# The closing stage of a hybrid convolution and MoE layer: last expert rows of two tiles read in two steps, and the sample tile summed ahead of tile 3

## The chip, the cores and the metric

One core of a Trainium2 chip runs the whole kernel. The metric is device time in microseconds of one execution, as the median of several runs. Five engines work side by side and wait for each other by semaphores: TensorE (PE), VectorE (DVE), ScalarE (ACT), GpSimd (POOL) and SyncE (SP). SP issues most DMA transfers, in the order of its program, and waits at an instruction until its semaphores allow it.

## The reference

The kernel computes one layer for 512 prompt tokens and 8 sample tokens, 1024 features wide: a token mixer of two convolution branches, then a mixture of 64 experts in which every token uses 8, and one shared expert. What matters here is the end of it:

```python
def moe_tokens(h, p):
    ...
    _, eidx = lax.top_k(jnp.where(emask, sel, -jnp.inf), TOP_K)
    w = jnp.take_along_axis(scores, eidx, axis=1)
    w = w / jnp.sum(w, axis=-1, keepdims=True) * ROUTED_SCALE
    ...
    act = jax.nn.silu(hg) * hu * gate[:, :, None].astype(h.dtype)
    routed = jnp.einsum('tef,efd->td', act, p['w2'])
    shared = (jax.nn.silu(h @ p['ws1']) * (h @ p['ws3'])) @ p['ws2']
    return routed + shared
...
    f = lax.map(lambda hs: moe_tokens(hs, p), h)
    x = x + gt2 * rmsnorm(f, p['g_post2'])
```

For each token, the outputs of its 8 experts are weighted and added, the shared expert's output is added, the sum is normalised by its root mean square, scaled by a gate and added to the residual.

## The kernel before

The 520 tokens make five tiles: tiles 0 to 3 of 128 prompt tokens, and tile 4 with the 8 sample tokens (`TT` is 5). The expert phase runs in passes. One pass takes two strips of 64 token rows, each of one expert: POOL gathers the rows, PE multiplies them with the expert's weights (L1746, L1754, L1760), ACT evicts the result (L973), and POOL scatters it to `y_rows` in DRAM (L624). The experts go in ascending order.

`y_rows` holds 8 rows for each token, in two halves. Half 0 of a tile holds its tokens' four latest choices (0 is the latest expert of a token, so the last to be computed) and half 1 its four earlier ones. A half of a full tile is 512 rows of 4 KB, 2 MB.

The closing stage brings them back and sums them. SP reads them in the order of its program, each read behind `rows_there(n)`, which loads a pass number from `few` and waits until that pass's rows have been written to DRAM: number 0 guards half 1 of all tiles, number 1 + i guards half 0 of tile i. The pass numbers are found in the routing: `last_of` collects the places of each tile's latest rows, PE transposes it and DVE takes the maximum (L1281, L1282, L1727, L1315, L1357). `y_first` are the buffers for half 1 and `y_last` those for half 0, in slots of the expert weights that are no longer needed (`slot_free(e)` waits for that). Tile 3's half 0 goes where tile 0's half 1 was, so it also waits for `early_pe`. `ysmp` takes the sample's 64 rows.

PE sums in PSUM. For the n-th tile in `order`, in the banks of `bank_of[n]`: `shared_down(n)` (L1819) adds the shared expert, `gated_rows(n, h, src)` (L1852) adds the four rows of half h with their gates, and `last_sums(n)` does so for half 0 as soon as it has landed. The sample's rows have a product of their own (L1878). Each full sum releases ACT (`stat_mm`): a square with a sum over columns (L1003) and a root (L1006). DVE takes the reciprocal (L1402), multiplies the sum in PSUM by it and by the gate (L1408, which counts `yacc`) and adds the residual (L1411, which counts `fin_out`). SP then stores the tile (L468). ACT, DVE and SP take the tiles in the order n = 0 to 4. `outb` has three buffers, so the fourth and the fifth tile wait for the stores of the first and the second.

Of the kernel before, what the change touches and what calls it, by code (L numbers as in the profile page):

```python
# [10 lines left out]
ALU = mybir.AluOpType  # L11
ACT = mybir.ActivationFunctionType
AX = mybir.AxisListType
ds = bass.ds

P = 128
# [6 lines left out]
def build_program(  # L23
# [8 lines left out]
    NP = x_prompt.shape[1]  # L32
    NS = x_sample.shape[0]
    T = NP + NS
# [4 lines left out]
    TT = (T + P - 1) // P  # L39
    LAST = T - (TT - 1) * P  # L40
    TOPK, NG, TOPG = 8, 8, 4
# [10 lines left out]
    y_rows = nc.dram_tensor("y_rows", (T * TOPK, D), F32, kind="Internal").ap()  # L52
# [4 lines left out]
    with ctx:  # L57
# [98 lines left out]
        y_first = [split] + [whole(t) for t in (slot_part(5, 0, YF), slot_part(0, 0, YF), slot_part(1, 0, YF))]  # L156
        y_last = [whole(t) for t in (slot_part(2, 0, YF), slot_part(3, 0, YF), slot_part(4, 0, YF))] + [split]
# [4 lines left out]
        ysmp = slot_part(3, YF + D, D)[0:NS * TOPK, :]  # L162
        outb = [hflat[:, D:2 * D], slot_part(4, YF, D), slot_part(4, YF + D, D)]

        ident = sb("ident", [P, P])
# [66 lines left out]
        first_at, steps_of, used_by, half_of, few = (table[:, n, :] for n in range(5))  # L232
        gidx = sb("gidx", [P, 8], I32)
        sidx = sb("sidx", [P, 6], I32)
        red = sb("red", [P, 4])
        nrm = sb("nrm", [P, 2, TT])
        last_of = nrm[:, :, :].rearrange("p a n -> p (a n)")[:, 0:1 + TT]
        kv = sb("kv", [P, TT, TOPK])
        m4 = sb("m4", [P, 4])
        bm = sb("bm", [P, P // 4])  # L240
# [2 lines left out]
        gcol, gpart_s, gcol_s, gmat_s = rs[:, 384:416], rs[0:NS * TOPK, 416:420], rs[0:NS * TOPK, 420:421], rs[0:NS * TOPK, 424:424 + NS]  # L243

        ps = ctx.enter_context(nc.psum_tensor("ps", [P, 8, 512], F32))
# [31 lines left out]
        S = {n: sem(n) for n in names}  # L277
# [2 lines left out]
        y_out = [sem(f"y_out{b}") for b in range(2)]  # L280
        y_first_in = sem("y_first_in")
        y_last_in = [sem(f"y_last_in{b}") for b in range(TT - 1)]
        order = tuple(range(TT))
        tile_out = [sem(f"tile_out{b}") for b in range(3)]
        g2_out, g2_in = sem("g2_out"), sem("g2_in")
        bank_of = (6, 0, 2, 4, 6)
        smp_in = sem("smp_in")

        LA = 7
# [8 lines left out]
        def _(sp):  # L298
# [119 lines left out]
            def tile_rows(dst, i, h, landed):  # L418

                at = i * P * TOPK + h * P * TOPK // 2  # L420
                for part, n in dst[i]:
                    sp.dma_start(part.rearrange("p (b d) -> p b d", b=n),
                                 y_rows[at:at + n * P, :].rearrange("(b p) d -> p b d", p=P)).then_inc(landed, 16)
                    at += n * P
# [8 lines left out]
            def rows_there(n):  # L433

                passes_gone = sp.value_load(few[0:1, 4 + n:5 + n], min_val=4, max_val=STEPS + 3)
                sp.wait_ge(S["yb_free"], passes_gone)
                passed()
# [9 lines left out]
            x1_back(TT - 1)  # L447
            sp.wait_ge(g2_out, 16)
            sp.dma_start(G2, g2_rows[0:1, :].to_broadcast([P, D])).then_inc(g2_in, 16)
            rows_there(1)  # L450
            tile_rows(y_last, 0, 0, y_last_in[0])
            slot_free(E - 2)
            sp.dma_start(G2s, g2_rows[1:NSEQ, :]).then_inc(g2_in, 16)
            rows_there(2)
            tile_rows(y_last, 1, 0, y_last_in[1])
            rows_there(3)
            slot_free(E - 1)
            tile_rows(y_last, 2, 0, y_last_in[2])
            rows_there(4)
            sp.wait_ge(S["early_pe"], 1)  # L460
            tile_rows(y_last, 3, 0, y_last_in[3])
            rows_there(TT)
            sp.dma_start(ysmp, y_rows[NP * TOPK:T * TOPK, :]).then_inc(smp_in, 16)
            for n in range(TT):
                i = order[n]
                sp.wait_ge(S["fin_out"], n + 1)
# [542 lines left out]
        def _(dve):  # L1009
            counts = {}  # L1010

            def link(ins, name=None, wait=True):

                key = name or "dve_step"
                counts[key] = counts.get(key, 0) + 1
                ins.then_inc(S[name] if name else dve_step, 1)
                if wait:
                    dve.wait_ge(S[name] if name else dve_step, counts[key])

            tt, ts, stt = dve.tensor_tensor, dve.tensor_scalar, dve.scalar_tensor_tensor  # L1020
# [47 lines left out]
            with dve.Fori(0, C // 2) as it:  # L1068
                for jj in range(2):
                    j = it * 2 + jj  # L1070
                    n = [0]
# [139 lines left out]
            for i in range(2, TT):  # L1211
                n, b = (P if i < TT - 1 else LAST), (0, 2, 6, 0, 2)[i]
# [13 lines left out]
            gs, g8, gi, gm, gneg, t8, wk8, wsum, wk9, val8 = (s8(n) for n in range(10))  # L1226
# [4 lines left out]
            for i in range(TT):  # L1231
                for q in range(NG):
                    link(dve.max(out=top[:, q, 8 * i:8 * i + 8], in_=sel[:, i, q * EG:(q + 1) * EG]),
                         wait=(i == TT - 1 and q == NG - 1))
# [5 lines left out]
            for i in range(TT):  # L1240
                link(dve.match_replace(out=gm[:, i, :], in_to_replace=g8[:, i, :], in_values=gs[:, i, :], imm_value=2 * NEG),
                     wait=(i == TT - 1))
# [5 lines left out]
            for i in range(TT):  # L1248
                link(dve.match_replace(out=repl[:, i, :], in_to_replace=t8[:, i, :], in_values=selm[:, i, :], imm_value=2 * NEG),
                     wait=(i == TT - 1))  # L1250
# [29 lines left out]
            link(ts(below, incl, 1.0 / STRIP, slotid[:, 0:1], ALU.mult, ALU.is_le))  # L1280
            link(dve.tensor_reduce(last_of[:, 0:1], val8[:, :, 4], AX.X, ALU.max), wait=False)  # L1281
            link(dve.tensor_copy(last_of[:, 1:1 + TT], val8[:, :, 0]), wait=False)  # L1282
            link(dve.tensor_reduce(first_strip, below, AX.X, ALU.add))
            link(ts(first_strip, first_strip, E - 1.0, None, ALU.min), "es_dve")
            dve.wait_ge(S["idx_mm"], 1)
# [26 lines left out]
            link(ts(one64[0:1, :], beyond, RING - 1.5, 2.0 * R, ALU.is_gt, ALU.mult))  # L1312
            link(ts(beyond, beyond, 1.0, float(SLOT), ALU.add, ALU.mult))
            link(tt(first_at, beyond, one64[0:1, :], ALU.add), "table_dve")
            link(dve.tensor_reduce(red[0:1 + TT, 2:3], ps[0:1 + TT, 6, 0:P], AX.X, ALU.max), "early_dve", wait=False)  # L1315
            tile_no = dve.alloc_register("tile_no")
            dve.reg_mov(tile_no, 0)

# [33 lines left out]
                              in_=xgs[u].rearrange("p (g r k) -> p g k r", g=4, k=C)[:, :, 4 * h:4 * h + 4, :]).then_inc(S["xe_dve"], 1)  # L1352

            dve.wait_ge(S["es_pe"], 2)
            last_pass = few[:, 4:5 + TT]
            link(ts(last_pass, ps[0:1, 6, P:P + 1 + TT], 4.0 * P - 1.0, None, ALU.add), "early_dve")
            link(ts(last_pass, last_pass, 7, None, ALU.logical_shift_right), "last_pass_dve", wait=False)  # L1357
            dve.wait_ge(S["sh_mm"], 2 * FT)
            for h in range(2):
# [37 lines left out]
            for n in range(TT):  # L1397
                i, f = order[n], bank_of[n]
# [15 lines left out]
        def _(pe):  # L1414
            def mark(ins, name):
                ins.then_inc(S[name], 1)

            mm, tr = pe.matmul, pe.transpose
            pe.wait_ge(consts, 12)
            pe.wait_ge(crow_in, 48)  # L1420
            for c in range(C):
                ins = tr(ps[:, 5, c * NS:(c + 1) * NS], x_stok[:, c * P:(c + 1) * P], ident[0:NS, 0:NS])
            mark(ins, "xs_pe")
            pe.wait_ge(S["csilu_act"], 1)
            for c in range(C):
                ins = tr(ps[:, 4, c * NSEQ:(c + 1) * NSEQ], c_tok[:, c * P:(c + 1) * P], ident[0:NSEQ, 0:NSEQ])
            mark(ins, "cT_pe")
            pe.wait_ge(x_in, 16)
            for c in range(C):
                if c >= 4:  # L1430
                    pe.wait_ge(S["xT_act"], c - 4 + 1)
                for i in range(TT - 1):
                    ins = tr(ps[:, c % 4, i * P:(i + 1) * P], x_tok[:, i, c * P:(c + 1) * P], ident[:, :])
# [8 lines left out]
            for c in range(C):  # L1442
                pe.wait_ge(S["xsq_dve"], c + 2)
                ins = quarter_stat(6, hT[:, c, :], c)
# [279 lines left out]
                             stop=(i == TT - 1 and k == TOPK - 1))  # L1724
            ins.then_inc(S["idx_mm"], 1)
            pe.wait_ge(S["es_dve"], 1)
            mm(ps[0:1 + TT, 6, 0:P], last_of, ident[:, :], start=True, stop=True)  # L1727
            mm(ps[0:1, 6, 3 * P:4 * P], red[:, 0:1], ident[:, :], start=True, stop=True).then_inc(S["es_pe"], 1)
            pe.wait_ge(S["hx_done"], TT)
            pe.wait_ge(S["idx_dve"], 1)  # L1730
# [31 lines left out]
                return ins  # L1762

            pe.wait_ge(S["early_dve"], 1)
            mm(ps[0:1, 6, P:P + 1 + TT], red[0:1 + TT, 2:3], ident[0:1 + TT, 0:1 + TT], start=True, stop=True).then_inc(S["es_pe"], 1)
            at_step = pe.alloc_register("step_pe")
            pe.reg_mov(at_step, 0)
            entries = table[:, :, :].rearrange("a n e -> a (n e)")
# [44 lines left out]
            def shared_down(n):  # L1813

                i, f = order[n], bank_of[n]
                rows = P if i < TT - 1 else LAST
                for h in range(2):
                    for k in range(FT):
                        mm(ps[0:rows, f + h, :], scr[:, 2 + k, i * P:i * P + rows], ws2_in[k][:, h * 512:(h + 1) * 512],  # L1819
                           start=(k == 0), stop=False)  # L1820
# [24 lines left out]
            def gated_rows(n, h, src):  # L1845

                i, f = order[n], bank_of[n]
                for c in range(2):
                    for b in range(4):
                        part, n = src[i][0] if b < src[i][0][1] else src[i][1]  # L1850
                        at = b % n * D + c * 512
                        ins = mm(ps[32 * b:32 * b + 32, f + c, :], gmat[:, b, i, h, :], part[:, at:at + 512],  # L1852
                                 start=False, stop=(h == 0))
                return ins

            def last_sums(n):
                pe.wait_ge(y_last_in[order[n]], 16 * len(y_last[order[n]]))
                mark(gated_rows(n, 0, y_last), "stat_mm")

            pe.wait_ge(S["gm_dve"], 2)  # L1860
# [1 line left out]
            pe.wait_ge(y_first_in, 16 * TT)  # L1862
            mark(gated_rows(0, 1, y_first), "early_pe")
            gated_rows(1, 1, y_first)
            pe.wait_ge(S["xe_dve"], passes * 2 + 2)
            last_sums(0)
            pe.wait_ge(S["ex_yd"], passes + 2)
            shared_down(3)
            last_sums(1)
            gated_rows(2, 1, y_first)  # L1870
            last_sums(2)
            gated_rows(3, 1, y_first)
            pe.wait_ge(S["yacc"], 1)
            shared_down(TT - 1)
            last_sums(TT - 2)
            pe.wait_ge(smp_in, 16)
            for c in range(2):
                ins = mm(ps[0:NS, bank_of[TT - 1] + c, :], gmat_s, ysmp[:, c * 512:(c + 1) * 512], start=False, stop=True)  # L1878
            mark(ins, "stat_mm")


_INS = ['x_prompt', 'x_sample', 'state_sconv', 'state_cconv', 'c_prompt', 'c_sample', 'w_ada', 'b_ada',
# [23 lines left out]
```

## Time and profile before

| | before |
|---|---|
| median of 3 runs | 1244.65 us |
| lowest and highest run | 1244.25 and 1246.88 us |
| the profiled execution | 1245.29 us |
| its span, first to last instruction | 1243.5 us |
| TensorE busy | 1170.2 us, 94% |
| VectorE, ScalarE, GpSimd busy | 45%, 26%, 42% |
| mean granted TensorE clock | 0.975 of full speed |

The profile is of one execution; the medians come from runs without it. Times in its rows count from the span's start. A busy share is a mean over stages of different kinds, so the last 35 us are read from their own rows. The durations of matmuls overlap, since they are pipelined: what a block costs is the time from its start to the start of the next.

### The profile page before, as it was taken

To read this page: it belongs to the slowest core of one execution; us is meant where nothing else is said; L and a number is where in the kernel's file an instruction comes from. 1 tells how busy PE (TensorE), PEld (TensorE's weight loads), DVE (VectorE), ACT (ScalarE), POOL (GpSimd) and SP (SyncE) were. 2 spreads that over 40 slices of the span, in tenths; PEclk is the share of its full clock that TensorE was granted. 3 is DMA by queue.
4 is the path that set the end of the run, shared out by engine and by line. 5 is a ranking of instruction groups with operands and counts; after the bars stand their busy time and mean duration, and the time that the engine had idled before them with its cause. 6 is when DMAs were issued, how large, how long until landed. Compare 5 with 4: busy or idle time off the path is not lost.

```text
span 1243.5 us, 26196 instructions
## 1 busy us (share of the span) xinstructions
PE 1170.2 (94%) x9253; PEld 848.0 (68%) x9254; DVE 562.0 (45%) x912; ACT 327.3 (26%) x620; POOL 523.6 (42%) x527
## 2 busy tenths in 40 slices
PE   4899999999999899979899999997989999899897
PEld 3699999999999899967655555554445555455442
DVE  3285667658568868127733422221112222222134
ACT  3523322322333441335211111111111111111122
POOL 2144444445448244310654445443344454354420
PEclk9899999999999899988999999998989999999999
DMA  9954344424421232437779999999999999999977
GB/s 313 323 168 153 99 137 152 151 85 152 152 84 34 69 101 88 133 142 307 288 283 391 392 393 413 411 412 416 413 414 411 410 414 401 412 414 413 352 288 271
DMA packets 149033, 337.45 MB, mean 271 GB/s; under 512 B 14807, under 2 KB 99363, under 8 KB 123369
## 3 DMA queue, kind: packets, MB, share of 16 engines
q1 hardware_dynamic: 129304, 296.57, 63.4%
q0 software_dynamic: 16656, 34.14, 7.3%
q10 hardware_dynamic: 3025, 6.07, 1.4%
q8 instruction: 34, 0.56, 0.2%
q14 instruction: 14, 0.11, 0.0%
HBM read 322.21 MB, written 33.30 MB: 286 GB/s over the span
## 4 chain that ended last, share of the span: by engine, by line
PE 73%; DMA 13%; DVE 6%; issue 5%; POOL 1%; SPq 1%; ACT 1%; DVEq 0%; POOLq 0%; ACTq 0%
PE ps L1746 24%; PE ps L1760 10%; DMA w<-in_w_dram 10%; PE ps L1509 10%; PE ps L1510 10%; PE ps L1511 10%; DMA ring<-in_w_ada_dram 2%; PE ps L1754 2%; PE ps L1819 1%; PE ps L1522 1%; PE ps L1852 1%; PE ps L1451 1%; PE ps L1527 1%; DVE sg L1152 1%; DVE rs L1129 1%
## 5 line engine op out<-in xcount | busy, mean ns | idle before, releaser
L1746 PE MATMUL ps<-w,xe 128*64 (+1 forms) x3136 | 381.1, 395 | 25.7 <-DMA w<-in_w_dram 20.2
L1746 PEld LDWEIGHTS ps<-w,xe 128*64 128x64 f32 x3136 | 223.3, 137 | 177.7 <-issue 63.2
L534 POOL TENSOR_TENSOR wsplit<-ring,wsplit 128x1024 fp32r<-128x1024 f32 x80 | 194.4, 2430 | 281.5 <-ACT wsplit L687 251.4
L1509 PE MATMUL ps<-h_s_hi,wsplit 128*128 128x260 f32 x960 | 272.2, 283 | 0.0
L1511 PE MATMUL ps<-h_s_hi,wsplit 128*128 128x260 f32 x960 | 270.7, 282 | 0.0
L1510 PE MATMUL ps<-h_lo_m_hi,wsplit 128*128 128x260 f32 x832 | 234.8, 282 | 0.0
L1371 DVE TENSOR_TENSOR rs<-sg,ps 128x128 f32<-128x128 f32 x98 | 28.2, 288 | 371.2 <-ACT sg L985 371.2
L1509 PEld LDWEIGHTS ps<-h_s_hi,wsplit 128*128 128x128 f32 x960 | 180.6, 188 | 6.7 <-issue 5.9
L1760 PE MATMUL ps<-w,eactT 128*64 128x512 f32 (+1 forms) x784 | 185.0, 592 | 0.0
L1511 PEld LDWEIGHTS ps<-h_s_hi,wsplit 128*128 128x128 f32 x960 | 180.8, 188 | 0.0
L687 ACT ACTIVATE wsplit<-ring 128x1024 fp32r<-128x1024 f32 x80 | 84.8, 1060 | 296.8 <-PE ps L1511 286.5
L1510 PEld LDWEIGHTS ps<-h_lo_m_hi,wsplit 128*128 128x128 f32 x832 | 156.6, 188 | 0.0
L1098 DVE SCALAR_TENSOR_TENSOR ps<-conv,vecs,ps 128x512 f32<-128x512 f32 x224 | 154.7, 745 | 0.0
L613 POOL DMA_INDIRECT conv<-h_rows,gidx x100 | 101.8, 1018 | 44.4 <-issue 24.6
L613 POOL DMA_INDIRECT scr<-h_rows,gidx x100 | 101.6, 1016 | 42.8 <-issue 22.9
L1760 PEld LDWEIGHTS ps<-w,eactT 128*64 128x64 f32 x784 | 54.3, 136 | 64.6 <-issue 54.1
L608 POOL COPY gidx<-tail 128x4 int32 (+1 forms) x50 | 10.2, 205 | 186.8 <-DVE xe L1351 183.7
L973 ACT ACTIVATE act<-ps 128x1024 f32<-128x1024 f32 x50 | 51.2, 1024 | 115.5 <-PE ps L1760 112.6
L985 ACT ACTIVATE sg<-ps 128x128 f32<-128x128 f32 x98 | 27.2, 277 | 199.6 <-PE ps L1746 199.6
L987 ACT ACTIVATE eactT<-ps 128x128 f32<-128x128 f32 x98 | 27.2, 277 | 172.6 <-PE ps L1754 172.6
L1351 DVE STREAM_TRANSPOSE xe<-scr 128x512 f32<-128x512 f32 x50 | 55.9, 1120 | 35.3 <-PE ps L1746 31.3
L1351 DVE STREAM_TRANSPOSE xe<-conv 128x512 f32<-128x512 f32 x50 | 56.2, 1123 | 32.8 <-PE ps L1746 32.8
(333 smaller groups left out, 1343.9 us busy)
## 6 DMA issues: line engine op xcount, KB each, us to landing
w<-in_w_dram SPq DMA_DIRECT2D x192, 1024.0 KB, 22.5
ring<-in_w_in_dram SPq DMA_DIRECT2D x56, 512.0 KB, 3.8
ring<-in_w_ada_dram SPq DMA_DIRECT2D x8, 2048.0 KB, 8.8
ring<-in_w_ada_dram SPq DMA_DIRECT2D x8, 1024.0 KB, 12.5
ring<-y_rows SPq DMA_DIRECT2D x4, 2048.0 KB, 17.0
ring<-in_w_out_a_dram SPq DMA_DIRECT2D x8, 512.0 KB, 4.1
ring<-in_w_out_b_dram SPq DMA_DIRECT2D x8, 512.0 KB, 4.1
ring<-in_w_o_dram SPq DMA_DIRECT2D x8, 512.0 KB, 4.2
```

The lines of the kernel that those rows point to most:

```text
L534: pool.tensor_tensor(wsplit[:, b, 1], raw[raw_slot], wsplit[:, b, 0], ALU.subtract).then_inc(S["w_lo"], 1)
L613: pool.indirect_dma_start(out=xgs[u][:, g * QR:(g + 1) * QR], out_offset=None, in_=h2_rows.rearrange("t (q d) -> (t q) d", q=4), in_offset ...
L687: act.activation(wsplit[:, b, 0], raw[raw_slot], ACT.Copy).then_inc(S["w_hi"], 1)
L973: act.activation(yb[:, 1 - u, :], ps[:, 4:6, :].rearrange("p b n -> p (b n)"), ACT.Copy).then_inc(S["ex_yd"], 1)
L1098: chain(stt(out=acc[k % 2] if k != KC - 2 else cvj, in0=glu[:, k:k + NP], scalar=vecs[:, ds(j + (V_WC + 8 * k), 1)], in1=acc[k % 2], op0=A ...
L1351: dve.transpose(out=xe[:, 4 * h:4 * h + 4, :].rearrange("p k (g s) -> p g k s", g=4), in_=xgs[u].rearrange("p (g r k) -> p g k r", g=4, k= ...
L1371: tt(eact[:, cols], esil[:, cols], ps[:, 2 + f, P:2 * P], ALU.mult).then_inc(S["ex_mul"], 1)
L1509: mm(ps[:, bank + h, 0:HT], wsplit[:, b, 0, k, :], hi[:, k, p:q], start=(k == 0), stop=False)
L1510: mm(ps[:, bank + h, 0:HT], wsplit[:, b, 0, k, :], lo[:, k, p:q], start=False, stop=False)
L1511: ins = mm(ps[:, bank + h, 0:HT], wsplit[:, b, 1, k, :], hi[:, k, p:q], start=False, stop=(k == C - 1))
L1746: ins = mm(ps[a * STRIP:(a + 1) * STRIP, 2 + f, 0:2 * P], xe[:, k, a * STRIP:(a + 1) * STRIP], w[a][:, f, k], start=(k == 0), stop=(k == C ...
L1760: ins = mm(ps[a * STRIP:(a + 1) * STRIP, 4 + h, :], eactT[:, k, a * STRIP:(a + 1) * STRIP], w[a][:, k, h * 512:(h + 1) * 512], start=(k == ...
```

## The change

`EARLY` is 2: for tiles 0 and 1 the routing also records the place of each token's choice 2, so that SP has two pass numbers more (numbers 6 and 7 of `rows_there`). Half 0 of these two tiles is read by choice: `choice_rows(i, (2, 3))` reads choices 2 and 3 behind the new pass number, `choice_rows(i, (0, 1))` reads choices 0 and 1 behind the old one. Each choice is a transfer of its own, 128 rows of 4 KB to every fourth partition. The tiles' buffers end up as before.

The order of the finish becomes tiles 0, 1, 2, the sample, tile 3; the two change banks. PE adds tile 2's and tile 3's halves 1 at other places, adds the sample's rows behind tile 2's last sums, and ends with tile 3's last sums. SP reads the sample's rows ahead of tile 3's.

```diff
-        last_of = nrm[:, :, :].rearrange("p a n -> p (a n)")[:, 0:1 + TT]
+        EARLY = 2
+        MARKS = 1 + TT + EARLY
+        last_of = nrm[:, :, :].rearrange("p a n -> p (a n)")[:, 0:MARKS]
...
-        order = tuple(range(TT))
+        order = (0, 1, 2, TT - 1, TT - 2)
...
-        bank_of = (6, 0, 2, 4, 6)
+        bank_of = (6, 0, 2, 6, 4)
...
-            rows_there(1)
-            tile_rows(y_last, 0, 0, y_last_in[0])
+            def choice_rows(i, choices):
+
+                part, at = y_last[i][0][0], i * P * TOPK
+                for k in choices:
+                    sp.dma_start(part[k::TOPK // 2].rearrange("t (b d) -> t b d", b=4),
+                                 y_rows[at:at + P * TOPK // 2, :].rearrange("(b t k) d -> k t b d", b=4, k=TOPK // 2)[k]
+                                 ).then_inc(y_last_in[i], 16)
+
+            rows_there(1 + TT)
+            choice_rows(0, (2, 3))
             slot_free(E - 2)
             sp.dma_start(G2s, g2_rows[1:NSEQ, :]).then_inc(g2_in, 16)
+            rows_there(2 + TT)
+            choice_rows(1, (2, 3))
+            rows_there(1)
+            choice_rows(0, (0, 1))
             rows_there(2)
-            tile_rows(y_last, 1, 0, y_last_in[1])
+            choice_rows(1, (0, 1))
             rows_there(3)
             slot_free(E - 1)
             tile_rows(y_last, 2, 0, y_last_in[2])
+            rows_there(TT)
+            sp.dma_start(ysmp, y_rows[NP * TOPK:T * TOPK, :]).then_inc(smp_in, 16)
             rows_there(4)
             sp.wait_ge(S["early_pe"], 1)
             tile_rows(y_last, 3, 0, y_last_in[3])
-            rows_there(TT)
-            sp.dma_start(ysmp, y_rows[NP * TOPK:T * TOPK, :]).then_inc(smp_in, 16)
...
             link(dve.tensor_copy(last_of[:, 1:1 + TT], val8[:, :, 0]), wait=False)
+            link(dve.tensor_copy(last_of[:, 1 + TT:MARKS], val8[:, 0:EARLY, 2]), wait=False)
...
             def last_sums(n):
-                pe.wait_ge(y_last_in[order[n]], 16 * len(y_last[order[n]]))
+                i = order[n]
+                pe.wait_ge(y_last_in[i], 16 * (TOPK // 2 if i < EARLY else len(y_last[i])))
...
             gated_rows(1, 1, y_first)
+            gated_rows(2, 1, y_first)
             pe.wait_ge(S["xe_dve"], passes * 2 + 2)
             last_sums(0)
             pe.wait_ge(S["ex_yd"], passes + 2)
+            shared_down(4)
+            gated_rows(4, 1, y_first)
+            last_sums(1)
+            pe.wait_ge(S["yacc"], 1)
             shared_down(3)
-            last_sums(1)
-            gated_rows(2, 1, y_first)
             last_sums(2)
-            gated_rows(3, 1, y_first)
-            pe.wait_ge(S["yacc"], 1)
-            shared_down(TT - 1)
-            last_sums(TT - 2)
             pe.wait_ge(smp_in, 16)
             for c in range(2):
-                ins = mm(ps[0:NS, bank_of[TT - 1] + c, :], gmat_s, ysmp[:, c * 512:(c + 1) * 512], start=False, stop=True)
+                ins = mm(ps[0:NS, bank_of[3] + c, :], gmat_s, ysmp[:, c * 512:(c + 1) * 512], start=False, stop=True)
             mark(ins, "stat_mm")
+            last_sums(4)
```

PE's end in the kernel before, the first row of each block from tile 3's shared expert on. L1819 is a shared block, L1852 sums of four rows (`y_last_in` with a tile's number is the wait for half 0; the row without a wait is tile 3's half 1), L1878 the sample's rows:

```order
L1819 MATMUL ps<-act,scr 128x512 [waits ex_yd]
L1852 MATMUL ps<-ring,act 32x512 [waits y_last_in1]
L1852 MATMUL ps<-act 32x512 [waits y_last_in2]
L1852 MATMUL ps<-ring,act 32x512 x8
L1819 MATMUL ps<-act,scr 8x512 [waits yacc]
L1852 MATMUL ps<-act 32x512 [waits y_last_in3]
L1878 MATMUL ps<-ring,rs 8x512 [waits smp_in]
```

PE's end in the changed kernel, from the same block on; its lines 1834, 1867 and 1893 are the lines 1819, 1852 and 1878 of before:

```order
L1834 MATMUL ps<-act,scr 128x512 [waits ex_yd]
L1867 MATMUL ps<-ring,act 32x512 x8
L1867 MATMUL ps<-ring,act 32x512 [waits y_last_in1]
L1834 MATMUL ps<-act,scr 8x512 [waits yacc]
L1867 MATMUL ps<-act 32x512 [waits y_last_in2]
L1893 MATMUL ps<-ring,rs 8x512 [waits smp_in]
L1867 MATMUL ps<-act 32x512 [waits y_last_in3]
```

The sample's shared block now stands ahead of tile 2's last sums, and tile 3's last sums stand behind the sample's rows, at the end.

DVE's last two finishes in the kernel before, tile 3 and then the sample (8 rows):

```order
L1408 SCALAR_TENSOR_TENSOR act<-ps,nrm,ring 128x1024 [waits tile_out0,dve_step]
L1411 TENSOR_TENSOR act<-act,ring 128x1024 [waits yacc]
L1402 RECIPROCAL nrm<-nrm 8x1 [waits root_act]
L1408 SCALAR_TENSOR_TENSOR act<-ps,nrm,ring 8x1024 [waits tile_out1,dve_step]
L1411 TENSOR_TENSOR act<-act,ring 8x1024 [waits yacc]
```

The same place in the changed kernel:

```order
L1423 SCALAR_TENSOR_TENSOR act<-ps,nrm,ring 8x1024 [waits tile_out0,dve_step]
L1426 TENSOR_TENSOR act<-act,ring 8x1024 [waits yacc]
L1417 RECIPROCAL nrm<-nrm 128x1 [waits root_act]
L1423 SCALAR_TENSOR_TENSOR act<-ps,nrm,ring 128x1024 [waits tile_out1,dve_step]
L1426 TENSOR_TENSOR act<-act,ring 128x1024 [waits yacc]
```

The finish with 8 rows has changed places with tile 3's, and so have the two stores that follow them on SP.

## Rows read from the trace of the kernel before

**Rows 1.** Page: its first line, and the chain that ended last, by engine.
```profile
span 1243.5 us, 26196 instructions
PE 73%; DMA 13%; DVE 6%; issue 5%; POOL 1%; SPq 1%; ACT 1%; DVEq 0%; POOLq 0%; ACTq 0%
```
**Rows 2.** Chain of waits in order of time (start, us, what): two pieces.
```profile
1209.51 3.70 PE ps L1819 x8
...
1239.97 1.21 DVE act L1411
```
**Rows 3.** Timeline of PE, 1209 to 1236 us: start, busy us, instructions, idle before.
```profile
1209.51 3.70 PE L1819 MATMUL ps<-act,scr 128*128 128x512 f32 x8 [0.27 <-DVE rs L1395]
1213.14 3.64 PE L1852 MATMUL ps<-act 128*32 128x512 f32 x32
1216.60 1.90 PE L1852 MATMUL ps<-ring,act 128*32 128x512 f32 x16
1218.43 3.70 PE L1819 MATMUL ps<-act,scr 128*128 128x512 f32 x8
...
1228.95 3.17 PE L1819 MATMUL ps<-act,scr 128*8 128x512 f32 x7
1231.53 0.63 PE L1852 MATMUL ps<-act 128*32 128x512 f32 x3
...
1234.20 1.88 PE L1878 MATMUL ps<-ring,rs 64*8 64x512 f32 x4
```
**Rows 4.** Line L422, loads issued at 1211.1, 1220.9, 1181.0: each with its landing.
```profile
L422 SPq DMA_DIRECT2D act<-y_rows x1: 360/360/360, 1211.1 to 1211.1; - x1
DMA to landing us min/median/max: 12.5/12.5/12.5
...
L422 SPq DMA_DIRECT2D act<-y_rows x1: 487/487/487, 1220.9 to 1220.9; - x1
DMA to landing us min/median/max: 8.4/8.4/8.4
...
L422 SPq DMA_DIRECT2D ring<-y_rows x1: 1330/1330/1330, 1181.0 to 1181.0; - x1
DMA to landing us min/median/max: 22.6/22.6/22.6
```
**Rows 5.** Timeline of ACT and DVE from 1234 us: tile 3, then the sample.
```profile
1234.35 1.02 ACT L1003 ACTIVATE scr<-ps 128x1024 f32<-128x1024 f32 x1 [5.42 <-PE ps L1852]
1236.03 1.28 DVE L1408 SCALAR_TENSOR_TENSOR act<-ps,nrm,ring 128x1024 f32<-128x1024 f32 x1
1238.67 1.27 DVE L1408 SCALAR_TENSOR_TENSOR act<-ps,nrm,ring 8x1024 f32<-8x1024 f32 x1
1239.97 1.21 DVE L1411 TENSOR_TENSOR act<-act,ring 8x1024 f32<-8x1024 f32 x1
```
**Rows 6.** Line L468, the five stores, and SP's wait at the end.
```profile
L468 SPq DMA_DIRECT2D out_dram<-act x5: 332/333/380, 1222.9 to 1241.2; - x5
DMA to landing us min/median/max: 2.6/3.1/8.5
...
SPq L472 <- DMA out_dram<-act: 1.5, 1, 1.5
```
**Rows 7.** Timeline of SP, its last issues ahead of tile 2's load.
```profile
1188.91 0.34 SPq L449 DMA_DIRECT2D ring<-g_rows  x1
1200.23 0.37 SPq L422 DMA_DIRECT2D ring<-y_rows  x1
1201.37 0.32 SPq L453 DMA_DIRECT2D ring<-g_rows  x1
1209.30 0.38 SPq L422 DMA_DIRECT2D ring<-y_rows  x1
```
**Rows 8.** Timeline of DVE in the routing: the copy, and what waits behind it.
```profile
607.38 0.16 DVE L1282 COPY nrm<-act 128x5 f32<-128x5 f32 x1
...
608.10 0.23 DVE L1286 COPY tok<-ps 128x66 f32<-128x66 f32 x1 [0.25 <-PE ps L1723]
```

More of the change, by code:

```diff
@@ L1314, in _ @@
             link(tt(first_at, beyond, one64[0:1, :], ALU.add), "table_dve")
-            link(dve.tensor_reduce(red[0:1 + TT, 2:3], ps[0:1 + TT, 6, 0:P], AX.X, ALU.max), "early_dve", wait=False)
+            link(dve.tensor_reduce(red[0:MARKS, 2:3], ps[0:MARKS, 6, 0:P], AX.X, ALU.max), "early_dve", wait=False)
             tile_no = dve.alloc_register("tile_no")
@@ L1354, in _ @@
             dve.wait_ge(S["es_pe"], 2)
-            last_pass = few[:, 4:5 + TT]
-            link(ts(last_pass, ps[0:1, 6, P:P + 1 + TT], 4.0 * P - 1.0, None, ALU.add), "early_dve")
+            last_pass = few[:, 4:4 + MARKS]
+            link(ts(last_pass, ps[0:1, 6, P:P + MARKS], 4.0 * P - 1.0, None, ALU.add), "early_dve")
             link(ts(last_pass, last_pass, 7, None, ALU.logical_shift_right), "last_pass_dve", wait=False)
@@ L1726, in _ @@
             pe.wait_ge(S["es_dve"], 1)
-            mm(ps[0:1 + TT, 6, 0:P], last_of, ident[:, :], start=True, stop=True)
+            mm(ps[0:MARKS, 6, 0:P], last_of, ident[:, :], start=True, stop=True)
             mm(ps[0:1, 6, 3 * P:4 * P], red[:, 0:1], ident[:, :], start=True, stop=True).then_inc(S["es_pe"], 1)
@@ L1764, in _ @@
             pe.wait_ge(S["early_dve"], 1)
-            mm(ps[0:1, 6, P:P + 1 + TT], red[0:1 + TT, 2:3], ident[0:1 + TT, 0:1 + TT], start=True, stop=True).then_inc(S["es_pe"], 1)
+            mm(ps[0:1, 6, P:P + MARKS], red[0:MARKS, 2:3], ident[0:MARKS, 0:MARKS], start=True, stop=True).then_inc(S["es_pe"], 1)
             at_step = pe.alloc_register("step_pe")
```

## Prediction

> **What bounds the kernel now.** I read the page's head first: of the chain that ended last TensorE holds 73% and the DMA 13% [rows 1]. That is an average over a projection stage, the routing, 49 expert passes and a closing stage. The change touches little outside the last stage, so only that stage counts. The chain of waits in order of time shows it as one stretch: a PE block that starts at 1209.51 us, after the last expert pass, and then PE to the very end of its own work, followed by ScalarE and VectorE [rows 2]. From 1209.51 us on no row of the chain is a DMA.
>
> The timeline of PE gives that stretch block by block [rows 3]. The reader is to see that each block starts where the one before it ends: the shared expert of one tile (L1819, 8 matmuls) takes 3.63 us from start to start, a half of four expert rows (L1852, 16 matmuls) 3.46 / 2 = 1.73 us, or 1.83 us when a shared block follows (1216.60 to 1218.43). The sample tile's shared block and the sums behind it take 5.25 us together (1228.95 to 1234.20), although the sample has 8 rows: its matmuls cost the same 0.43 us each as those of a full tile. Then the sample's own rows, 4 matmuls, 1.88 us with their end. No block names a DMA as what it waited for. The first block starts when VectorE has made the gate matrix, which the change leaves alone.
>
> Were the loads late, it would show there. They are close but not late. Tile 2's last rows were issued at 1211.1 us and landed 12.5 us later, at 1223.6; PE took them up at 1225.5, which is 1.73 + 1.73 us ahead of 1228.95. The second piece of tile 3's last rows went at 1220.9 and landed 8.4 us later, at 1229.3; its first sums stand at 1231.53 [rows 3, 4]. So in the kernel before the loads have some 2 us in hand.
>
> Behind PE stands the finish of a tile: a square-sum and a root on ScalarE, then a reciprocal and two passes over 1024 columns on VectorE (L1408, L1411). For tile 3 ScalarE starts at 1234.35 and L1408 at 1236.03, 1.68 us later. The sample's L1408 starts 2.64 us after that and its L1411 ends at 1241.18 (1239.97 + 1.21) [rows 5]. The sample's finish is as long as a full tile's, because it is as many columns wide. Its output of 32 KB is issued at 1241.2; the issue takes 0.33 us and SP waits 1.5 us more [rows 6]: 1.8 us from issue to landing.
>
> **The change part by part.** *The reads in two steps.* SP gets eight loads of 512 KB for tiles 0 and 1 in place of two of 2 MB, so six issues more, of 0.37 us like the one at 1200.23, and two more looks at a pass number, at most 0.77 us each (1200.23 + 0.37 to 1201.37, which holds another wait too): 3.8 us of SP in all. They lie where SP waits anyway, between 1188.91 and 1209.30 [rows 7]; only the two issues of tile 1's later half stand right ahead of tile 2's load, 0.4 us. What moves: 1 MB of tile 0 and 1 MB of tile 1 may be read before 1209 us instead of around it. If none of it went earlier, the loads would land as they did, and those were in time. Tile 0's last sums stand at 1218.3 us now (below), so a half read as late as 1201.4 and landing in 12.5 us is still in time. So the edit frees transfers that no instruction waited for: its gain is 0, and the cover that hides its cost is SP's idle time. If that cover were gone, tile 2's load would go 3.8 us later and land at 1227.4.
>
> *The order on PE.* The same blocks run in another order, so PE's sum stays, but for one more step from sums to a shared block (0.1 us). From 1209.51: shared tile 2 3.63, three first halves 5.19, tile 0's last sums 1.83, shared tile 3 3.63, its first half 1.73, tile 1's last sums 1.83, the sample's shared block with tile 2's last sums 5.25. That is 1232.60. Then the sample's rows 1.72 (4 x 0.43) to 1234.3 and tile 3's last sums to 1236.0, 1236.2 with their end. Every load is wanted later than before: tile 2's at 1230.9 instead of 1225.5, tile 3's at 1234.3 instead of 1231.5. The sample's shared block waits for VectorE to have read tile 0's bank. Tile 0's sums end at 1220.2, 1.7 us of ScalarE and 1.3 us of L1408 behind that is 1223.2, and the block stands at 1227.3, so this wait costs 0.
>
> *The finish.* Here the order costs. Before, tile 2 is done by the time tile 3's sums end, and two finishes queue on VectorE. Now tile 2's sums, the sample's and tile 3's end at 1232.6, 1234.3 and 1236.2, 1.7 to 1.9 us apart, and each finish takes 2.64 us. Three of them queue. ScalarE starts 0.15 us after the next block does (1234.20 to 1234.35), so tile 2's L1408 stands at 1232.60 + 0.15 + 1.68 = 1234.43, the sample's at 1237.07, tile 3's at 1239.71. Its L1411 ends 2.51 us after that (1238.67 to 1241.18 in the row of before): 1242.22, against 1241.18. **That is +1.0 us.** Tile 3's root is ready at 1237.9, so VectorE, not PE, sets the end. The bound below: if nothing queued ahead of tile 3, its L1408 would start at 1236.2 + 1.68 and the end would be 1240.4, a gain of 0.8 us. I take +1.0, since all three durations are rows.
>
> *The last output.* The last store is now tile 3's 512 KB instead of the sample's 32 KB. The shortest landing among the five outputs, 2.6 us, is that of tile 3 in the kernel before, with no load beside it; the median is 3.1 us [rows 6]. Against 1.8 us that is +0.8 us, at most +1.3 us; I take **+0.8 us**, the one alone on the queue. The Trainium skill (DMA: Bandwidth & Descriptors, section "Anatomy of one DMA — SWDGE (gpsimd) path") gives a fit of 2.0 us plus the bytes at 436 GB/s, for another way of issuing; by that estimate the two stores take 3.2 and 2.1 us, the difference is 1.1 us, and the sum would be 0.3 us higher. The row decides.
>
> *The third part* is a copy of two more columns of the routing (about as long as L1282, 0.16 us), and two rows more in a transpose and a maximum. VectorE idles 0.25 us for PE right behind that place [rows 8], so it costs 0, at most 0.2 us.
>
> **Sum.** +1.0 + 0.8 = +1.8 us on a span of 1243.5 us: 1245.3 us. The profiled execution took 1245.29 us with its span and all around it, so 1247.1 us in its terms. It lay 0.64 us above the median of the runs, 1244.65 us, so the median to expect is **1246.4 us**. Two times of this kernel within 0.2%, 2.5 us, can't be told apart with confidence, and +1.8 us lies within that.
>
> **The rivals.** *A: the small loads land late (slower).* The place is tile 1's last sums, wanted at 1225.5, whose later half can't be issued before 1209.3. It decides if that half needs more than 16 us. For it: each of the small loads writes only every fourth partition, a shape that the trace of before does not have, and one load of the same rows needed 22.6 us when issued at 1181.0 with others ahead [rows 4]; that would stall PE by 6.4 us and give 1252.8 us. Against it: 1 MB is half of what landed in 12.5 us in the same crowd, and 2 MB fewer stand around it. The Trainium skill speaks for it (DMA: Bandwidth & Descriptors, "Measured (HBM→SBUF, 128 partitions, SWDGE, issued from GpSimd)"): it asks for at least 1 MiB a load for three quarters of the peak, and the trace of before shows no landing of a 512 KB load beside others by which to tell whether that holds here. 7 in 100.
>
> *B: the loads were the limit after all (faster).* Two us in hand are little, and in runs without a profile PE may have waited for tile 2's or tile 3's rows. A wait of 3 us now gone, less the 1.8 us, gives 1243.4 us. For it: landings of 8.4 to 12.5 us vary by more than the 2 us in hand. Against it: the runs without a profile are no slower than the profiled one. 12 in 100; beyond 0.2% it would need 4.3 us of hidden waiting.
>
> *C: the change does nothing (same).* The three finishes don't queue, because tile 2's sums come out earlier than I place them or the stores hide their length: -0.8 + 0.8 = 0, 1244.7 us. Against it stands the 2.64 us of each finish. 14 in 100.
>
> *Forecast:* VectorE's queue and the longer store. Its own range is 1245.8 us (the sum less the 0.6 us by which profiled run and median differ) to 1247.2 us (1.0 + 1.3 + 0.2). 67 in 100.
>
> **How the numbers follow.** Of the forecast's 67, some 17 fall above +0.2%, since +1.8 us lies 0.7 us below that line and the executions of the kernel before differ by 2.6 us; the rest is within. A's 7 go to slower; B gives 6 to faster and 6 to same; C's 14 are same, but for 2 of scatter on the faster side. Faster 0.08, same 0.68, slower 0.24. The range from 1243.6 to 1248.6 us takes in C, most of B's, and the forecast with its scatter.
>
> **What would show it.** Right: PE without a DMA wait from 1209.5 us on, its last matmul at the same time within 0.3 us; three L1408 on VectorE 2.64 us apart; tile 3's store last, landing 2.6 us after its issue. The forecast is wrong if PE's blocks show gaps behind a load, if the last matmul ends over 1 us earlier or later than 1236, or if the start at 1209.5 itself moves.

## The result, and the profile after

The changed kernel takes 1247.59 us as the median of 20 runs, against 1245.21 us for the kernel before in 20 runs beside it. The ratio is 1.0016 with a 95% interval from 1.0009 to 1.0023: some 2.0 us slower, between 1.1 and 2.9 us, clear of zero, about 0.16%. The forecast was 1.8 us, 1246.4 us on the median known then, and no change that a single measurement of this kernel could tell. That median, of three runs, lay 0.56 us below the one of the 20 runs beside; with it the forecast's own range of 1245.8 to 1247.2 us lies low, and the measured median falls 0.4 us above it.

The profiled execution of the changed kernel lasted 1249.99 us, with a span of 1248.3 us, and so lay 2.4 us above the median of its kernel. The 4.8 us between the two spans are not what is to be explained. A better measure is the **tail**: from the start of PE's first shared block after the last pass to the end of the span. It is 33.99 us before (1243.5 - 1209.51) and 35.85 us after (1248.3 - 1212.45): **1.86 us more**. The other 2.94 us lie ahead of it, and more than half of them ahead of the first instruction that the change adds. The timeline of VectorE in the routing of the changed kernel:

```profile
609.13 0.16 DVE L1296 COPY nrm<-act 128x5 f32<-128x5 f32 x1
609.20 0.16 DVE L1297 COPY nrm<-act 128x2 f32<-128x2 f32 x1
```

The first row is the copy of [rows 8], at 609.13 instead of 607.38 us, already 1.75 us late. The second is the added copy, and it starts 0.07 us behind the first. Nine other profiles (below) begin their tails anywhere from 1207.96 to 1210.74 us, with the added copy and without it. Two of them, the short last store and the cut finish, run the changed kernel's program up to the tail, and start it at 1210.74 and 1209.82 us: the late start belongs to this execution and not to the change.

The timeline of PE in the tail, to be held against [rows 3] (L1834, L1867 and L1893 are the lines 1819, 1852 and 1878 of before):

```profile
1212.45 3.70 PE L1834 MATMUL ps<-act,scr 128*128 128x512 f32 x8 [0.27 <-DVE rs L1410]
1216.08 3.64 PE L1867 MATMUL ps<-act 128*32 128x512 f32 x32
1219.54 3.62 PE L1867 MATMUL ps<-ring,act 128*32 128x512 f32 x32
1223.09 3.70 PE L1834 MATMUL ps<-act,scr 128*128 128x512 f32 x8
1226.72 3.64 PE L1867 MATMUL ps<-ring,act 128*32 128x512 f32 x32
1230.18 3.17 PE L1834 MATMUL ps<-act,scr 128*8 128x512 f32 x7
1232.76 0.63 PE L1867 MATMUL ps<-act 128*32 128x512 f32 x3
...
1235.42 1.88 PE L1893 MATMUL ps<-ring,rs 64*8 64x512 f32 x4
1237.23 1.92 PE L1867 MATMUL ps<-act 128*32 128x512 f32 x16
```

No block waits for a DMA, and the last one ends at 1239.15, 26.70 us after the tail's start; the working of the prediction gave 26.7. What follows it is the timeline of ACT and DVE, against [rows 5]:

```profile
1237.25 1.28 DVE L1423 SCALAR_TENSOR_TENSOR act<-ps,nrm,ring 128x1024 f32<-128x1024 f32 x1
1239.22 1.02 ACT L1017 ACTIVATE scr<-ps 128x1024 f32<-128x1024 f32 x1 [0.45 <-PE ps L1867]
1239.89 1.27 DVE L1423 SCALAR_TENSOR_TENSOR act<-ps,nrm,ring 8x1024 f32<-8x1024 f32 x1
1242.52 1.28 DVE L1423 SCALAR_TENSOR_TENSOR act<-ps,nrm,ring 128x1024 f32<-128x1024 f32 x1
1243.83 1.23 DVE L1426 TENSOR_TENSOR act<-act,ring 128x1024 f32<-128x1024 f32 x1
```

Three finishes, 2.64 and 2.63 us apart: tile 2, the sample, tile 3. ACT starts on tile 3 at 1239.22, so its first pass could stand at 1240.9 (1.68 us later); it stands at 1242.52, because VectorE is busy with the sample. VectorE ends at 1245.06 (1243.83 + 1.23), 32.61 us into the tail, against 31.67 before. The rest, from there to the end of the span, is 3.24 us against 2.32: SP's waits show the landing of the last store, against the 1.5 us of [rows 6].

```profile
SPq L486 <- DMA out_dram<-act: 2.3, 1, 2.3
```

### The profile page after: what moved, and what is told of

It is laid out like the page before. It is cut to its first block, busy times and chain, and to the rows that moved or that the text cites. A ratio compares the mean times of both kernels' runs of the same rounds, so it can differ in the third digit from the quotient of the medians.

```text
span 1248.3 us, 26211 instructions
## 1 busy us (share of the span) xinstructions
PE 1174.6 (94%) x9253; PEld 848.6 (68%) x9254; DVE 561.9 (45%) x913; ACT 327.4 (26%) x620; POOL 524.9 (42%) x527
## 4 chain that ended last, share of the span: by engine, by line
PE 73%; DMA 12%; DVE 6%; issue 5%; POOL 2%; ACT 1%; SPq 1%; DVEq 0%; POOLq 0%; ACTq 0%
PE ps L1761 24%; PE ps L1775 10%; DMA w<-in_w_dram 10%; PE ps L1524 10%; PE ps L1525 9%; PE ps L1526 9%; DMA ring<-in_w_ada_dram 2%; PE ps L1769 2%; PE ps L1834 1%; PE ps L1537 1%; PE ps L1466 1%; PE ps L1867 1%; PE ps L1542 1%; DVE sg L1166 1%; POOL wsplit L548 1%
## 5 line engine op out<-in xcount | busy, mean ns | idle before, releaser
L1775 PE MATMUL ps<-w,eactT 128*64 (+1 forms) x784 | 184.9, 592 | 0.0
L987 ACT ACTIVATE act<-ps 128x1024 f32<-128x1024 f32 x50 | 51.2, 1024 | 115.5 <-PE ps L1775 112.6
## 6 DMA issues: line engine op xcount, KB each, us to landing
w<-in_w_dram SPq DMA_DIRECT2D x192, 1024.0 KB, 22.6
```

Of the source, the lines that this page charges most:

```text
L987: act.activation(yb[:, 1 - u, :], ps[:, 4:6, :].rearrange("p b n -> p (b n)"), ACT.Copy).then_inc(S["ex_yd"], 1)
L1775: ins = mm(ps[a * STRIP:(a + 1) * STRIP, 4 + h, :], eactT[:, k, a * STRIP:(a + 1) * STRIP], w[a][:, k, h * 512:(h + 1) * 512], start=(k == ...
```

## The experiments

All are read by the tail. The last two columns split it: up to the end of VectorE's last pass, and from there on. A row is one execution; the ratios below are of several runs of each kernel and of the kernel before beside them, with a 95% interval.

| kernel | span | tail starts | tail | to VectorE's end | rest |
|---|---|---|---|---|---|
| before | 1243.5 | 1209.51 | 33.99 | 31.67 | 2.32 |
| before, again | 1243.9 | 1209.88 | 34.02 | 31.67 | 2.35 |
| changed | 1248.3 | 1212.45 | 35.85 | 32.61 | 3.24 |
| reads only | 1244.6 | 1210.59 | 34.01 | 31.67 | 2.34 |
| order only | 1245.5 | 1209.67 | 35.83 | 32.61 | 3.22 |
| changed, short last store | 1245.7 | 1210.74 | 34.96 | 32.61 | 2.35 |
| changed, sample's finish cut | 1244.0 | 1209.82 | 34.18 | 30.99 | 3.19 |
| sample last | 1247.7 | 1207.96 | 39.74 | 37.33 | 2.41 |
| sample last, old reads | 1249.3 | 1209.94 | 39.36 | 37.01 | 2.35 |
| POOL adds tile 3 | 1243.9 | 1209.98 | 33.92 | 31.38 | 2.54 |

**The reads alone.** The changed kernel with the order, the banks, PE's sequence and the place of the sample's read of before; the last two are left out of the cut:

```diff
-        order = (0, 1, 2, TT - 1, TT - 2)
+        order = tuple(range(TT))
...
-        bank_of = (6, 0, 2, 6, 4)
+        bank_of = (6, 0, 2, 4, 6)
...
```

> The two-step reads alone, in the order of the kernel before. Measure: the tail, from the start of the first shared block after the last pass to the end of the span; 33.99 us before (1243.5 - 1209.51), 35.85 us in the changed kernel (1248.3 - 1212.45). Theory (the cost is the order of the finish, and the reads moved nothing that was waited for): tail 34.0 us within 0.3, ratio to before 1.000. Rival (the reads disturb the last passes or land late, and that is the cost): tail above 35, or the last passes above 11.2 us each, ratio 1.0015 or more. Second rival (loads bounded the kernel before): tail 33 or less.

Measured: tail 34.01 us, ratio 0.9997 (0.9988 to 1.0006). The tail's first block and VectorE's last pass:

```profile
1210.59 3.70 PE L1834 MATMUL ps<-act,scr 128*128 128x512 f32 x8 [0.27 <-DVE rs L1410]
```
```profile
1241.05 1.21 DVE L1426 TENSOR_TENSOR act<-act,ring 8x1024 f32<-8x1024 f32 x1
```

In this order the reads in two steps neither cost nor gain anything that can be told.

**The order alone.** The changed kernel with the reads of before (`EARLY` is 0, and the added copy is left out):

```diff
-            rows_there(1 + TT)
-            choice_rows(0, (2, 3))
+            rows_there(1)
+            tile_rows(y_last, 0, 0, y_last_in[0])
...
-            rows_there(2 + TT)
-            choice_rows(1, (2, 3))
-            rows_there(1)
-            choice_rows(0, (0, 1))
             rows_there(2)
-            choice_rows(1, (0, 1))
+            tile_rows(y_last, 1, 0, y_last_in[1])
```

> The new order alone (sample finished ahead of tile 3, on PE, ACT, DVE and SP), with the 2 MB reads of the kernel before. Theory: the whole cost stays, tail 35.9 us within 0.3, three finishes 2.64 us apart on DVE and no PE block waiting for a load, ratio 1.0015. Rival (the reads carry the cost): tail 34.0. A rival on the loads (the order needs the early reads): gaps ahead of tile 2's or tile 1's last sums on PE, tail above 36.5.

Measured: tail 35.83 us, ratio 1.0019 (1.0010 to 1.0028). The whole cost is in the order, and this order did not need the early reads: PE's last two blocks follow each other without a gap, and the three finishes queue on VectorE as in the changed kernel.

```profile
1232.64 1.88 PE L1880 MATMUL ps<-ring,rs 64*8 64x512 f32 x4
1234.45 1.92 PE L1854 MATMUL ps<-act 128*32 128x512 f32 x16
```
```profile
1234.47 1.28 DVE L1410 SCALAR_TENSOR_TENSOR act<-ps,nrm,ring 128x1024 f32<-128x1024 f32 x1
1237.10 1.27 DVE L1410 SCALAR_TENSOR_TENSOR act<-ps,nrm,ring 8x1024 f32<-8x1024 f32 x1
1239.73 1.28 DVE L1410 SCALAR_TENSOR_TENSOR act<-ps,nrm,ring 128x1024 f32<-128x1024 f32 x1
```

**The store by itself.** The changed kernel, with the last store cut to 8 rows; 120 rows of tile 3 are not stored.

```diff
-                sp.dma_start(dst, outb[n % 3][0:P if i < TT - 1 else LAST, :]).then_inc(tile_out[n % 3], 16)
+                rows = LAST if n >= TT - 2 else P
+                sp.dma_start(dst[0:rows, :], outb[n % 3][0:rows, :]).then_inc(tile_out[n % 3], 16)
```

> The changed kernel, but its last store, tile 3's, is cut to 8 rows (the other 120 rows of tile 3 are left out of the output). Theory: the store's length is worth 0.8 us of the tail, so the tail falls from 35.85 to 35.0 us, with DVE's last pass where it was, 32.6 us after the tail's start. Rival (the store's length is hidden, the landing is all latency): tail 35.8 us.

Measured: tail 34.96 us, VectorE's end unmoved at 32.61. The store's length is 0.89 us of the 1.86. In SP's waits the landing is back at what it was before:

```profile
SPq L487 <- DMA out_dram<-act: 1.5, 1, 1.5
```

**The queue by itself.** The changed kernel, with VectorE's two passes for the sample over 8 columns; the other columns of the sample's output are left out.

```diff
-                stt(out=buf, in0=ps[0:rows, f:f + 2, :].rearrange("p b n -> p (b n)"), scalar=r, in1=(G2 if i < TT - 1 else G2s)[0:rows, :],
+                w = D if i < TT - 1 else 8
...
+                stt(out=buf[:, 0:w], in0=acc, scalar=r, in1=(G2 if i < TT - 1 else G2s)[0:rows, 0:w],
...
-                tt(buf, buf, x1b[i][0:rows, :], ALU.add).then_inc(S["fin_out"], 1)
+                tt(buf[:, 0:w], buf[:, 0:w], x1b[i][0:rows, 0:w], ALU.add).then_inc(S["fin_out"], 1)
```

> The changed kernel, but DVE's two passes for the sample run over 8 columns instead of 1024 (the rest of the sample's output is left out), so that only two full finishes queue ahead of the end. Theory: tile 3's first pass starts when its root is ready, 1.68 us behind ACT's start, so the end comes 1.8 us earlier, not a whole finish of 2.64 us: tail 34.0 us. Rival (PE or ACT sets the end, not DVE's queue): tail 35.8 us. Rival (the queue is worth a whole finish): 33.2 us.

Measured: tail 34.18 us, 1.67 us less, of which 1.62 us are VectorE's end (32.61 to 30.99). The timeline of VectorE shows what ends the wait now: it idles for ACT's root ahead of tile 3, as it would with no queue.

```profile
1237.51 0.15 DVE L1431 TENSOR_TENSOR act<-act,ring 8x8 f32<-8x8 f32 x1
1238.07 0.16 DVE L1417 RECIPROCAL nrm<-nrm 128x1 f32<-128x1 f32 x1 [0.41 <-ACT nrm L1020]
1238.26 1.28 DVE L1428 SCALAR_TENSOR_TENSOR act<-ps,nrm,ring 128x1024 f32<-128x1024 f32 x1
```

**The sample last.** If two finishes that queue are the cost, the sample's shared block (3.4 us of PE) could stand between them. The changed reads with the old order of tiles; tile 2's half 1 is added ahead of tile 0's last sums, as in the changed kernel. On PE, held against the sequence of before from there on:

```diff
             shared_down(3)
             last_sums(1)
-            gated_rows(2, 1, y_first)
+            gated_rows(3, 1, y_first)
             last_sums(2)
-            gated_rows(3, 1, y_first)
-            pe.wait_ge(S["yacc"], 1)
-            shared_down(TT - 1)
             last_sums(TT - 2)
+            pe.wait_ge(S["yacc"], 1)
+            shared_down(TT - 1)
```

> Two-step reads, and the sample last: its shared block moved behind tile 3's last sums, so that tile 3's finish is over on DVE when the sample's begins. Theory: PE's work ends as late as before, the sample's finish starts at once and its short store follows: 0.8 us less than before, tail 33.2 us; tile 3's last sums are wanted 19.5 us after the tail's start and land 19.5 us after it in the changed kernel, so up to 0.4 us of waiting may be added. Ratio to before 0.9994. Rival (DVE's queue is not what the end hangs on): tail 34.0 or more.

Measured: tail 39.74 us, ratio 1.0021 (1.0011 to 1.0030): the tail is 6.5 us longer than expected, and not through VectorE. The timeline of PE, and then the windows around the gap (the columns are the window's length, busy time on PE, PEld, DVE, ACT and POOL, the granted clock, the DMA share and GB/s):

```profile
1225.68 1.90 PE L1867 MATMUL ps<-act 128*32 128x512 f32 x16
1230.96 3.64 PE L1867 MATMUL ps<-act 128*32 128x512 f32 x16 [3.38 <-DMA act<-y_rows]
1234.38 4.90 PE L1834 MATMUL ps<-act,scr 128*8 128x512 f32 x8
1239.21 1.88 PE L1894 MATMUL ps<-ring,rs 64*8 64x512 f32 x4
```
```profile
1228.00:1230.00 2.00, 0.00 (x0) 0.00 (x0) 1.27 (x3) 1.05 (x3) 0.00 (x0) 1.00 0.54 219
1230.00:1231.00 1.00, 0.04 (x4) 0.04 (x6) 0.97 (x2) 0.00 (x0) 0.00 (x0) 0.58 0.61 250
1231.00:1234.40 3.40, 3.40 (x17) 0.71 (x18) 0.86 (x1) 0.00 (x0) 0.00 (x0) 0.50 0.46 181
1234.40:1239.20 4.80, 4.80 (x12) 0.78 (x7) 2.67 (x3) 1.41 (x3) 0.00 (x0) 0.73 0.01 3
```

PE asked for tile 3's last rows at 1227.40 (1225.68 + 1.72), 19.4 us into the tail, and got them at 1230.96. While it idled the granted clock fell to 0.50, the lower of its two levels, 1.2 GHz, and it was back only some 6 us into the new work (3.4 us at 0.50, then 4.8 us at a mean of 0.73, of which 2.6 us at 0.50 make that mean; read in steps of 1 us, the clock is 0.51 up to 1237.0 and 1.00 behind it): the 16 matmuls took 3.42 us from start to start instead of 1.72, the shared block 4.83 instead of some 3.5. A gap of 3.56 us cost 3.6 + 1.7 + 1.3 = 6.6 us. The load's own row tells that it came late:

```profile
L424 SPq DMA_DIRECT2D act<-y_rows x2: 374/427/480, 1219.3 to 1219.8; - x2
DMA to landing us min/median/max: 7.8/9.5/11.2
```

The second piece landed 11.2 us after its issue, at 1231.0, where I had counted on the 7.8 us of the changed kernel's profile.

This is one execution, and one of the longer ones: it lies 2.0 us above the median of its 11 runs. The ratio of the runs is worth 2.6 us (1.4 to 3.7), against 5.75 us between the tails (39.74 - 33.99). So the stall is not of this length in every run; how long it is in the others is not shown.

**The sample last, with the old reads.** The same, with the reads replaced as in the order alone.

> As the kernel with the sample last, but with the 2 MB reads of before. Tile 3's last sums are wanted 19.5 us after the tail's start; tile 3's rows landed 19.8 us after it in the kernel before. Theory: here the reads first have something to hide, 0.3 to 0.8 us: tail 33.5 to 34.0 us, with a wait for a load ahead of tile 3's last sums. Rival (the reads never matter): tail equal to that of the kernel with two-step reads within 0.1 us.

Measured: tail 39.36 us, ratio 1.0034 (1.0021 to 1.0046). The same gap ahead of the same block:

```profile
1232.61 3.64 PE L1854 MATMUL ps<-act 128*32 128x512 f32 x16 [3.05 <-DMA act<-y_rows]
```

Both numbers expected were wrong, since both versions stall. The two tails, of one execution each, show no worth of the early reads. The runs do: with them the median is 1247.35 us (11 runs), with the old reads 1249.85 us (6 runs), and each of the six lies above eight of the eleven. So in this order, where PE does wait for a load, the reads in two steps gain some 2 us. Which wait becomes shorter by it, no trace shows.

**POOL adds tile 3.** The kernel before, with tile 3's residual add on POOL, which SP waits for ahead of tile 3's store:

```diff
-                tt(buf, buf, x1b[i][0:rows, :], ALU.add).then_inc(S["fin_out"], 1)
+                if n != TT - 2:
+                    tt(buf, buf, x1b[i][0:rows, :], ALU.add).then_inc(S["fin_out"], 1)
...
+            pool.wait_ge(S["yacc"], TT - 1)
+            buf = outb[(TT - 2) % 3]
+            pool.tensor_tensor(buf, buf, x1b[TT - 2], ALU.add).then_inc(S["turn_pool"], 1)
```

> The kernel before, in which POOL, idle at the end, does tile 3's residual add, so that DVE takes up the sample as soon as its root is ready. Theory (the queue on DVE sets the end, the loads don't): sample's first pass 0.9 us earlier; tile 3's add takes 2.4 to 2.5 us on POOL (128 x 1024 took 2.43 us there in the projection stage) and its store then ends last: tail 33.4 to 33.6 us, against 33.99. Rival (a queue on DVE of one pass is hidden by the stores): tail 34.0 us.

Measured: tail 33.92 us, where 33.4 to 33.6 was expected, ratio 0.9993 (0.9984 to 1.0002): no gain that can be told. The timelines of DVE and of POOL say why:

```profile
1238.30 1.27 DVE L1415 SCALAR_TENSOR_TENSOR act<-ps,nrm,ring 8x1024 f32<-8x1024 f32 x1
1239.61 1.75 DVE L1419 TENSOR_TENSOR act<-act,ring 8x1024 f32<-8x1024 f32 x1
```
```profile
1237.94 2.34 POOL L683 TENSOR_TENSOR act<-act,ring 128x1024 f32<-128x1024 f32 x1 [25.05 <-DVE act L1415]
```

The sample's first pass came 0.84 us earlier, as meant (28.32 us into the tail; 29.16 by [rows 5]). But its second pass, two inputs from SBUF, took 1.75 us instead of 1.21 with POOL's add beside it, which ended 0.67 us into it, at 1240.28 (1237.94 + 2.34). The first pass, which reads PSUM, kept its 1.27 us. The Trainium skill (Perfetto Trace Analysis, "Optimizing Scalar/DVE Operations") says that the two engines share a read port of SBUF, so that moving work between them may not help. This trace agrees, with 0.54 us lost; the port itself is not seen in it. Another 0.22 us went in the rest behind VectorE's end (2.54 against 2.32), for a cause that is not shown.

**The kernel before, again.** No edit.

> The kernel before once more, for a second profile. Tail 34.0 us within 0.1 if no load comes late; the tail's start, 1209.5 us in the first profile and 1208.0 to 1212.5 us in the kernels so far, shows how far two executions differ ahead of the closing stage. If the load of tile 3's last rows lands more than 22.0 us after the tail's start, PE stalls and the tail is over 34.3 us.

Measured: tail 34.02 us; it starts at 1209.88. The tail repeats to 0.03 us, its start does not.

## Why the prediction was right

*The reads in two steps: gain 0.* Shown by the reads alone and, from the other side, by the order alone, for orders in which PE waits for no load; with the sample last it did not hold. Two sizes in this step were off without consequence. A small load took SP about 0.6 us to issue, not 0.37 us, and the landings of the changed kernel's eight ran from 5.0 to 17.5 us, as the rows of tile 1's earlier half show (line L456):

```profile
L456 SPq DMA_DIRECT2D ring<-y_rows x2: 577/1134/1692, 1195.4 to 1196.0; - x2
DMA to landing us min/median/max: 7.5/12.5/17.5
```

*The order on PE: the same sum, and no wait.* 26.70 us where 26.7 was worked out. That it fits to 0.01 us is luck: the blocks up to the sample's rows took 22.97 us instead of 23.09, and the sample's rows 1.81 us instead of 1.72. *The finish: +1.0 us.* VectorE's end moved by 0.94 us (32.61 - 31.67), in the changed kernel and in the order alone alike. That the queue does it is shown by the kernel with the sample's finish cut: 1.62 us came off VectorE's end, where the prediction's working left 1.8 us between tile 3's root and its turn, and the row of ACT 1.62 us (1242.52 - 1240.90). *The last output: +0.8 us.* 0.92 us between the rests (3.24 - 2.32), 0.89 us by the cut store. The row of a lone 512 KB store gave 0.8. The estimate from the Trainium skill's fit (DMA: Bandwidth & Descriptors, "Anatomy of one DMA — SWDGE (gpsimd) path"), for another way of issuing, gave 1.1; the measurement lies between. *Sum:* 0.94 + 0.92 = 1.86 us, against 1.8. The mechanism is right in both terms; that the sums agree so closely is luck too, since the worked-out 1.04 us (1242.22 - 1241.18) was 0.10 us too much and the 0.8 us 0.12 us too little.

Of the signs named, one seems to speak against the forecast: the start at 1209.5 did move, to 1212.45. The nine other starts show that it moves from one execution to the next. The others held: no wait for a DMA, VectorE's three rows, and the landings of the stores, 2.6 us in every one that the profile gives, tile 3's last one among them:

```profile
L482 SPq DMA_DIRECT2D out_dram<-act x5: 333/342/351, 1227.5 to 1245.1; - x5
DMA to landing us min/median/max: 2.6/2.6/2.6
```

*Rival A*, late small loads, did not occur: tile 1's later half was issued at 1210.6 and 1211.2, landed 5.0 and 7.5 us later, and was wanted at 1228.4. One of the eight did need more than 16 us (17.5), but it was issued at 1196.0, 32 us before it was wanted. The prediction says under this rival that the trace of before has no 512 KB load beside others. It has one: tile 3's second piece, issued 0.4 us behind the first one of 1.5 MB, with the landing of 8.4 us of [rows 4]. *Rival C* is excluded by the three rows 2.64 us apart. *Rival B*, loads that bound the kernel before, is the one that the prediction treated too lightly. It spoke of some 2 us in hand. Over the profiles, tile 3's last rows landed this long after the tail's start: 19.8 and 20.2 us (before, twice), 18.9 (reads only), 21.7 (POOL adds tile 3), 19.6 (changed), 21.9 (order only), 20.8 and 22.3 (short store, finish cut), 23.0 and 22.6 (sample last). The order of before wants them at 22.0 us, the changed order at 24.8. So the margin in the order of before was 0.3 to 3.1 us where it was seen (1.8 to 3.1 us for tile 2's rows, wanted at 16.0), none of its four profiles stalled, but later landings do occur in its neighbours; the changed order buys 2.8 us of margin for its 1.9 us. And the price of a stall was set too low: rival A's 6.4 us counted the wait alone, where the sample-last kernel's profile shows some 6.5 us paid for a wait of 3.6. Whether some runs of the kernel before stall is not shown.

## What to carry to other kernels

When the engines behind the last producer take longer per tile than the producer, the order of the tiles sets how many finishes queue: count them, and put the piece with the shortest store last. Moving a load that nobody waits for gains nothing, but before its slack is spent on a new order, take its landing from several executions, and charge a stall of TensorE with the slow clock behind it too. When two profiles differ ahead of the changed place, compare the stretch itself; and hold a stretch of one execution against the runs, as the sample-last kernels show.

## What the runs showed of the hardware

After the wait of 3.56 us for a load TensorE's granted clock stood at 0.50, and it stayed there for some 6 us of the work that followed; the 16 matmuls of four expert rows took 3.42 us in it instead of 1.72. One engine slowed another that worked on other data: VectorE's 8 x 1024 add went from 1.21 to 1.75 us with POOL's add beside it, while POOL's took 2.34 us, no more than the 2.43 us of the projection stage. And loads of 128 rows of 4 KB to every fourth partition were not slow to land: the pair issued around 1211 us took 5.0 and 7.5 us, and tile 3's 512 KB piece to all partitions took 7.8 us in the same profile.
